# Where the last modulation slabs are computed in a two-layer trunk: two pairs to the second attention, one pair of each attention to its end, lambda arithmetic later in the head

## The reference

```
def layer(x, cond, p, l, angles, ctx):
    mod = jax.nn.silu(cond) @ p['w_mod'][l] + p['b_mod'][l]          # 1024 x 6144 per layer
    sh1, sc1, g1, sh2, sc2, g2 = jnp.split(mod, 6, axis=-1)
    h = rms_norm(x, p['norm1'][l]) * (1.0 + sc1) + sh1
    mixed, ctx_out = token_mixers(h, p, l, angles, ctx)   # attention, linear attention, diff. attention, gated merge
    x = x + g1 * mixed
    h = rms_norm(x, p['norm2'][l]) * (1.0 + sc2) + sh2
    a, u = jnp.split(h @ p['w_ffn_in'][l], 2, axis=-1)
    x = x + g2 * ((jax.nn.silu(a) * u) @ p['w_ffn_out'][l])
# in the differential attention: p = softmax1 - lam * softmax2
#   lam = exp(sum(lp[0]*lp[1])) - exp(sum(lp[2]*lp[3])) + lam_init
```

## Time and profile before

| what | value |
|---|---|
| median of three runs | 2388.95 us (2387.24 to 2390.85) |
| the profiled execution | 2387.86 us, its span 2386.1 us |
| PE busy | 2310.7 us, 97% of the span |
| DVE busy | 1495.4 us, 63% |
| ACT busy | 1065.7 us, 45% |
| DMA | 224.01 MB, mean 94 GB/s |
| granted TensorE clock | 0.992 of full |

### The profile page before, as it was taken

The page is one execution under the profiler, slowest core; times in us unless marked ns, Lnnn a source line. Parts: engine busy times, 40 slices in busy tenths (PEclk is TensorE's granted clock), DMA queues, the critical chain, the costliest instruction groups (busy, mean ns, idle before and its releaser), DMA issues. The chain is left out here.

```text
span 2386.1 us, 40526 instructions
## 1 busy us (share of the span) xinstructions
PE 2310.7 (97%) x16311; PEld 2139.7 (90%) x16311; DVE 1495.4 (63%) x2403; ACT 1065.7 (45%) x2121; POOL 194.7 (8%) x160
## 2 busy tenths in 40 slices
PE   7999999899999999999999999999999999999999
PEld 5877877799999999999997777778999999999998
DVE  5335568677664865747643565787676658467473
ACT  5433357644442642524346333674444345344252
POOL 1330000100003000000215200010000110000000
PEclk9999999999999999999999999999999999999999
DMA  9225440122225223232231163102222432323222
GB/s 299 96 68 172 143 152 28 45 80 80 75 94 159 63 79 88 81 98 68 93 125 53 51 199 120 33 1 71 80 80 80 159 81 73 105 62 98 65 73 84
DMA packets 246666, 224.01 MB, mean 94 GB/s; under 512 B 6945, under 2 KB 232305, under 8 KB 245969
## 3 DMA queue, kind: packets, MB, share of 16 engines
q1 hardware_dynamic: 242528, 219.25, 29.7%
q0 software_dynamic: 480, 0.66, 0.3%
q10 hardware_dynamic: 3472, 1.52, 0.2%
HBM read 211.70 MB, written 9.70 MB: 93 GB/s over the span
## 5 line engine op out<-in xcount | busy, mean ns | idle before, releaser
L2352 ACT ACTIVATE ring_high<-raw 128x512 fp32r<-128x512 f32 (+1 forms) x278 | 158.1, 609 | 250.0 <-PE ps L2706 150.4
L2492 DVE TENSOR_TENSOR ring_low<-raw,ring_high 128x512 fp32r<-128x512 f32 (+1 forms) x278 | 204.5, 761 | 69.3 <-ACT ring_high L2352 65.1
L2771 PE MATMUL ps<-hH,ring_low 128*128 128x320 f32 x640 | 197.9, 309 | 0.3
L2771 PE MATMUL ps<-hH,ring_high 128*128 128x320 f32 x640 | 197.8, 309 | 0.0
L2771 PE MATMUL ps<-hL,ring_high 128*128 128x320 f32 x640 | 197.8, 309 | 0.0
L1564 DVE SCALAR_TENSOR_TENSOR xT<-ps,mod,xT 128x512 f32<-128x512 f32 (+1 forms) x128 | 64.0, 545 | 193.4 <-PE ps L2706 193.4
L359 PE MATMUL ps<-wH,hL 128*128 128x512 f32 (+1 forms) x460 | 176.5, 384 | 5.2 <-DVE wL L871 2.6
L359 PE MATMUL ps<-wH,hH 128*128 128x512 f32 (+1 forms) x460 | 171.0, 372 | 0.0
L2706 PE MATMUL ps<-gH,ring_low 128*128 128x320 f32 x704 | 160.9, 310 | 0.3 <-DVE xT L1564 0.3
L2706 PE MATMUL ps<-gL,ring_high 128*128 128x320 f32 x704 | 160.4, 309 | 0.0
L2706 PE MATMUL ps<-gH,ring_high 128*128 128x320 f32 x704 | 160.3, 309 | 0.0
(11 more groups left out here) (384 smaller groups left out, 6194.8 us busy)
## 6 DMA issues: line engine op xcount, KB each, us to landing
raw<-in_w_in SPq DMA_DIRECT2D x56, 1024.0 KB, 5.4
raw<-in_w_ffn_in SPq DMA_DIRECT2D x88, 512.0 KB, 5.2
gmod<-in_w_mod SPq DMA_DIRECT2D x24, 1024.0 KB, 8.6
raw<-in_w_ffn_out SPq DMA_DIRECT2D x16, 1024.0 KB, 5.1
b_raw<-in_w_branch SPq DMA_DIRECT2D x22, 512.0 KB, 4.4
head_w<-in_w_mod SPq DMA_DIRECT2D x8, 1024.0 KB, 12.4
modw<-in_w_mod SPq DMA_DIRECT2D x8, 1024.0 KB, 7.6
raw<-in_w_out SPq DMA_DIRECT2D x8, 1024.0 KB, 5.8
```

The source lines that it names most:

```text
L2352: nc.scalar.activation(ring_block(m.ring_high, b, src.shape[1], src.shape[2]), src, ACT.Copy).then_inc(m.sem("w_high"), 1)
L2492: nc.vector.tensor_tensor(ring_block(m.ring_low, b, nk, cols), src, ring_block(m.ring_high, b, nk, cols).bitcast(F32), ALU.subtract).then_ ...
L2771: last = nc.tensor.matmul(m.ps[:, plan.banks[n, 0][BANK[what]], 0:HALF], w[:, k, :], a[:, k, :], start=(first and k == 0 and q == 0), stop ...
```

## The change

Four things. The lambda arithmetic moves on DVE and ACT from before slab 2 to before slab 3's place in the loop (its buffer `lpw` gets a place of its own). Layer 1's projections do slabs 8 to 15 only; slabs 16 to 19 become two pairs of layer 1's attention. Each attention ends with a pair (`mod_pair` after the last step) which it leaves in its bank; the merge copies it (`late_row`), turns it behind its first tile, and adds it on DVE before tile b1 may write that bank. So layer 0's fourth pair goes from step 16 to the end, and its turn chunks are (0, 1) at step 5 and (2) at step 11; layer 1 has pair 0 ahead of the steps, its turn at step 2, and pair 1 at the end. Buffers for six slabs instead of four.

```diff
-        self.modw = [at(f"modw{j}", [P, KT, W256], 61440 + (0, 8192, 32768, 40960)[j]) for j in range(4)]
+        self.modw = [at(f"modw{j}", [P, KT, W256], (61440, 69632, 94208, 102400, 0, 8192)[j]) for j in range(6)]
...
+def attention_mods(L):
+    return [(L + 1, slab) for slab in (0, 2, 4, 6)] if L + 1 < DEPTH else [(L, 16), (L, 18)]
...
-    mods = range(8, 20)
+    mods = range(8, 20 if more else 16)
...
-            if more:
-                sp.wait_ge(m.sem("low_ready"), n)
-                for j in range(2):
-                    sp.dma_start(m.modw[j][:, :, :], k_tiles(d["w_mod"], L + 1, j * W256, W256)
-                                 ).then_inc(m.sem(f"attention_mod{j}"), 16)
+            sp.wait_ge(m.sem("low_ready"), n)
+            layer, slab = attention_mods(L)[0]
+            for j in range(2):
+                sp.dma_start(m.modw[j][:, :, :], k_tiles(d["w_mod"], layer, (slab + j) * W256, W256)
+                             ).then_inc(m.sem(f"attention_mod{j}"), 16)
...
-    mod_at = {6 * p - 2: p for p in range(1, pairs)}
-    turn_at = {6 * p - 1: p // 2 for p in range(1, pairs, 2)}
+    pairs = attention_mods(L)
+    buffers = [(0, 1), (2, 3), (4, 5), (4, 5)] if more else [(0, 1), (4, 5)]
+    mod_at = {4: 1, 10: 2} if more else {}
+    turn_at = {5: (0, 1), 11: (2,)} if more else {2: (0,)}
...
+            pe.wait_ge(*freed(len(chunks) - 2))
+            mod_pair(len(pairs) - 1, len(chunks))
...
-            order.step(affine(nc, m, dve, order, L, 1))
             if more:
-                dve.wait_ge(*freed(max(turn_chunk.values())))
-                order.step(affine(nc, m, dve, order, L + 1, 0))
+                order.step(affine(nc, m, dve, order, L, 1))
+    return 6 + len(chunks) % 2
...
@@ merge, ACT @@
             highs(-1)
+            nc.scalar.activation(m.late_row[:, :], m.ps[:, late_bank, 0:W256], ACT.Copy).then_inc(m.sem("late_row"), 1)
             for g in plan.gates:
...
@@ merge, DVE, in the loop over tiles @@
+                    if g == 0 and what == 1:
+                        layer, slab = attention_mods(L)[-1]
+                        dve.wait_ge(m.sem("late_turned"), 1)
+                        summed_late = order.step(sum_mod(nc, m, late_bank, W256, 2, 2))
+                        dve.wait_ge(*summed_late)
+                        add_mod_bias(nc, m, layer, 2 * slab, 2).then_inc(m.sem("late_added"), 1)
+                        dve.wait_ge(m.sem("late_added"), 1)
+                        order.step(affine(nc, m, dve, order, layer, 0 if layer > L else 1))
...
@@ merge, PE @@
                         last.then_inc(m.sem("tile_done"), 1)
+                        if (g, c) == (0, 0):
+                            pe.wait_ge(m.sem("late_row"), 1)
+                            turn_mod(nc, m, m.late_row, late_bank, W256).then_inc(m.sem("late_turned"), 1)
                     for c in range(2):
+                        if (g, c) == (0, 1):
+                            pe.wait_ge(m.sem("late_added"), 1)
                         branch(g, c).then_inc(m.sem("tile_done"), 1)
...
@@ head, ACT @@
-                if n == 1:
+                if n == 3:
                     act.wait_ge(m.sem("lam_sums"), 1)
...
@@ head, DVE: the lambda lines become the function lambdas(), called later @@
             ahead = slabs_ahead(slabs)
             for n in range(N):
+                if n == 3:
+                    lambdas()
                 for x in ahead[n][0]:
```

More of the change, by code:

```diff
@@ L987, in _ @@
             sp.wait_ge(m.sem("caches"), 6 * 16)
-            if more:
-                for j in range(2):
-                    sp.wait_ge(m.sem(f"attention_mod{j}"), 16)
+            for j in range(2):
+                sp.wait_ge(m.sem(f"attention_mod{j}"), 16)
         @block.scalar
@@ L1205, in attention @@
     of_step.append([])
-    if more:
-        add_chunk(0, 0, None, 0, "act")
+    add_chunk(0, 0, None, 0, "act")
     first_mods = of_step.pop()
@@ L1268, in store_values, with load_pair @@
                              m.kv[:, 4:8, CTX, :]).then_inc(m.sem("v_stored"), 16)
[L1270 to L1280, removed]
+            def load_pair(p):
+                layer, slab = pairs[p]
+                for i, b in enumerate(buffers[p]):
+                    sp.dma_start(m.modw[b][:, :, :], k_tiles(d["w_mod"], layer, (slab + i) * W256, W256)
+                                 ).then_inc(m.sem(f"mod_loaded{b}"), 16)
+            for b in buffers[0]:
+                sp.sem_inc(m.sem(f"mod_loaded{b}"), 16)
+            for p in ((1, 2) if more else (1,)):
+                load_pair(p)
+            store_values(sp)
             for j in range(2):
-                next_load(sp, m, nxt, j, *(("slab_used", 2 * pairs - 3 + j) if more else ()))
+                next_load(sp, m, nxt, j, "slab_used", 2)
+            if more:
+                sp.wait_ge(m.sem("slab_used"), 6)
+                load_pair(3)
             next_loaded(sp, m, nxt)
@@ L1349, in mod_pair @@
             def mod_pair(p, c):
-                for i in range(2):
-                    j = 2 * p + i
-                    pe.wait_ge(m.sem(f"mod_loaded{j % 4}"), 16 * (j // 4 + 1))
-                    mod_groups(nc, m, m.modw[j % 4], 6 + c % 2, i).then_inc(m.sem("slab_used"), 1)
+                for i, b in enumerate(buffers[p]):
+                    pe.wait_ge(m.sem(f"mod_loaded{b}"), 16 * sum(b in x for x in buffers[:p + 1]))
+                    mod_groups(nc, m, m.modw[b], 6 + c % 2, i).then_inc(m.sem("slab_used"), 1)
             for c in first_mods:
@@ L1374, in _ @@
                     if turn is not None:
-                        pe.wait_ge(*freed(mod_chunk[2 * turn + 1]))
-                        for i in range(2):
-                            last = turn_mod(nc, m, m.mrow[:, 2 * turn + i, :], 6 + c % 2, i * W256)
+                        pe.wait_ge(*freed(mod_chunk[turn[-1]]))
+                        for i, p in enumerate(turn):
+                            last = turn_mod(nc, m, m.mrow[:, p, :], 6 + c % 2, i * W256)
                     if mod is not None:
@@ L1539, in _ @@
                         if turn is not None:
-                            done = order.step(sum_mod(nc, m, 6 + c % 2, 0, 4, 2))
+                            done = order.step(sum_mod(nc, m, 6 + c % 2, 0, 2 * len(turn), 2))
                             dve.wait_ge(*done)
-                            for i in range(2):
-                                ins = add_mod_bias(nc, m, L + 1, 8 * turn + 4 * i, 2, 8 * i)
+                            for i, p in enumerate(turn):
+                                ins = add_mod_bias(nc, m, pairs[p][0], 2 * pairs[p][1], 2, 8 * i)
                         if n:
@@ L3367, in program @@
             project_attention(nc, m, d, L)
-            attention(nc, m, d, L, (SLAB, lambda sp, j, sem: load_merge(sp, m, d, L, 0, 0, j, sem), 16))
-            merge(nc, m, d, L, (tail_slabs(False)[0], first_slabs, 16))
+            late_bank = attention(nc, m, d, L, (SLAB, lambda sp, j, sem: load_merge(sp, m, d, L, 0, 0, j, sem), 16))
+            merge(nc, m, d, L, (tail_slabs(False)[0], first_slabs, 16), late_bank)
             tail(nc, m, d, L)
```

39 lines of the change are left out of this document (21 added, 18 removed).

## The result

| | before | changed |
|---|---|---|
| median, us | 2388.55 (6 runs) | 2397.39 (6 runs) |
| lowest to highest | 2385.27 to 2390.85 | 2394.12 to 2399.24 |
| profiled execution: time, span | 2387.86, 2386.1 | 2396.26, 2394.5 |

The ratio is 1.0036, with a 95% interval of 1.0026 to 1.0046: the change makes the kernel 8.8 us slower by the medians, 8.4 by the profiled executions. The prediction of 2393.0 had the side right; its range ended at 2396.5. Measured once more in another set, the changed kernel took 2395.45 against 2389.77, a ratio of 1.0026 (1.0015 to 1.0036), 5.7 us slower.

What follows compares the result with a forecast made beforehand. PE's own work and its few waits bound the kernel (97% busy). Terms -4.8 - 2.1 + 6.8 - 1.6 - 0.65 + 6.7 = +4.35 us gave 2393.0, own range 2391 to 2395, with rivals 2389 to 2396.5.

Steps and rivals of the forecast that it cites:

- Head, -4.8: Between slabs 1 and 2, moving lambda removes PE's pause (3.3 us) and the half clock behind it (1.5).
- Merges, +6.8 and +6.7: Layers 0 and 1: PE waits for ACT's late copy, queued behind gate 1's load, with 1.5 us of half clock charged.
- the second new wait: In the merge, PE's wait at b1 for DVE's late addition; claimed not to bind (484.8 against 487.3 in layer 0).
- Projections of layer 1, -1.6: Two pairs go (3.9 us), but a late key store brings a new PE pause of 2.3, leaving 1.6.
- Attention of layer 1, -0.65: Pair 0 fills the pause of 2.19, gaining 1.15 us; the single turn at step 2 costs 0.5.
- Attention of layer 0, -2.1: Pair 3 and the double turn leave (2.6 us); a turn of one pair comes in at 0.5.
- The pair at the attention's end: A last pair of 1.93 us runs while DVE, ACT and POOL finish: costs nothing, at most 0.3 in layer 1.
- (a): Merges: the late copy is in time, costing only 0.35 each; 2377.5 to 2380.5, chance 0.08.
- (b): The clock stays up in the merges' pauses: 3.1 us less, 2390, chance 0.10.
- (c): The store isn't late in layer 1's projections: 2.3 us less, 2390.7, chance 0.13.
- (d): More is lost: slab 2's load late in the head, or turns 0.7 each and longer half clock; 2395 to 2396.5, chance 0.14.
- (e): Head: the lambda move does nothing, as another load holds ACT; +4.8 us, 2398, chance 0.05.

Runs made afterwards that it cites:

- experiment 4: Changed kernel with PE doing 36 discarded matmuls of tile (0,1) while it waits for the late row: 2396.42 us, ratio 1.0035; run again, 2395.36.
- experiment 3: Changed kernel with SP's first store of the differential keys issued ahead of the two modulation loads, both layers: 2391.78 us, ratio 1.0016.
- experiment 5: Changed kernel without the late pair's copy, transposes and DVE work in the merges (output not the reference's): 2382.04 us, ratio 0.9971.
- experiment 2: Changed kernel with only ACT's copy of the late row moved ahead of the blocks that wait for gate 1's load: 2399.66 us, ratio 1.0049.
- experiment 6: Changed kernel with DVE's late addition earlier, and either PE's turn behind tile (0,1) (2380.47 us) or ACT's copy ahead of gate 1's wait (2381.86).
- experiment 1: Kernel before with only the lambda move and its buffer `lpw`: 2384.86 us, ratio 0.9983.

## Why the prediction was right or wrong

The step that failed first is in the projections of layer 1: the pause that the store causes was charged its own length, and the half clock behind it was put at nothing. It follows in six of eight profiles and costs 1.6 us on average. The other misses are two sizes, the turn of one pair and the half clock in the merges, and a gain that was read from a single execution.

**Head, -4.8: right.** The pause went with lambda, 4.85 by the means and 4.3 by the medians of the edit alone. "All but some 0.1" was too sure: in three of twelve executions slab 2's load is late itself.

**Merges, +6.8 and +6.7: the mechanism right, the size low.** The copy ran right behind the two blocks, the pause was 6.26 and 6.29, and moving the copy and the addition took it away. The half clock was charged at the head's 1.5; behind these longer pauses it cost 2.6 and 2.1 on average (experiment 4). With the wait's own length that makes 7.7 and 7.15: 0.9 and 0.45 missed. How much it costs is partly chance: with pauses nearly as long, in experiment 3, the merges lost 6.5 and 6.8, about what was predicted. That the clock kept up in tile (0,0) gains nothing while PE waits anyway was right: it is 1.5 us once the wait is gone (experiment 5). That the second new wait doesn't bind was right as well, but only behind the first (experiment 2).

**Projections of layer 1, -1.6: the step that failed.** "A new pause of 2.3, and 1.6 is left of the gain": the pause came where it was said, for the reason that was said, with 2.58. But it was priced without half clock behind it, while the same text charged it for the merges and pointed to a pause of 2.19 that was followed by it. It follows in six of eight profiles. Over these eight the stage takes 185.4 on average, as the three profiles with the old projections do: nothing is left of the two pairs' 3.9 us. Like against like, both terms that were named are right. Without half clock in the stage it goes from 184.6 to 182.8 and 182.7, a gain of 1.8 to 1.9. With the store first it takes 181.9 and 182.2, against 185.6 and 185.9 before, all four with half clock behind the modulation's pause: 3.7 for the 3.9. Of the loss, the pause was foreseen and 1.6, on average, was not.

**Attention of layer 1, -0.65: the second step that failed.** The 1.15 was read from one profile, in which half clock stood behind the pause of 2.19. Two others with the old attention don't show it (132.4 long), and against these the stage, 133.4, costs 1.0. That pair 0 fits into the pause was right: the maxima up to the sixth stand where they stood. The 1.0 is the single turn, taken as 0.5 between 0 and 0.7 by halving a turn of two pairs. PE's transposes take 0.38, and behind them it waits 0.56 for DVE, which it doesn't behind a turn of two pairs (0.11 at most). Why only the single turn has this wait is open.

**Attention of layer 0, -2.1: 0.45 too much,** for the same price of the turn: there too the maxima behind it come 1.0 later. **The pair at the attention's end** cost under 0.1 in layer 1, where the last maximum comes 1.0 later and the stage is 1.0 longer; the bound was 0.3.

**The rivals.** (a) isn't what happened; experiment 6 made it true by moving the late pair's operations, and 2380.5 and 2381.9 are near its 2380.5. (b) falls: the clock fell in the merges' pauses in all three profiles with the late pair unmoved and PE idle. (c) falls, and the store does what was said. (d) comes nearest, and partly by other items than it named: it had the turns at 0.7 and a longer half clock, and lacked the one behind the store. Its 2396.5, the end of the whole range, lies 0.9 under the measured 2397.39; the other set's 2395.45 lies inside. That is the spread between sets and no merit of the sum, which was too low by 3.6 in the means of the stages. (e) falls by the head's stage and by experiment 1.

What the larger part of the five misses has in common is that it rests on what the clock did behind a pause in one execution; the rest, 0.45 to 0.5 in each attention, is the turn. The prediction charged the half clock where the pause was long, left it out where the pause was a by-product, and counted it as a gain where one profile happened to have it.

## What to carry to other kernels

An operation put behind a wait on its own queue can cost the engine that needs it the whole wait, however small it is; look on each engine for the idle stretch that it fits into, and check all the links of a chain (copy, turn, addition), since moving one alone uncovers the next wait; here two of the three had to move. A small store that something waits for is worth trying ahead of large loads on its queue. When a sum counts the half clock behind one pause, count it behind all, as a chance times its price, and take from several profiles which of the old pauses have it.

## What the runs showed of the hardware

Behind the same pause of some 1.9 us, at the same place of a projection, PE's clock fell in 9 of 26 cases (13 profiles, two layers; twice in layer 0, seven times in layer 1), at a price of 1.0 to 1.8 us each. Behind the pause of 2.19 at the start of the old attention of layer 1 it fell in one of three, behind the store's of 2.4 to 4.0 in six of eight, and behind the late row's of 6.0 to 6.3 in six of six. It also fell in 3 of 11 profiles early in layer 1's new attention, behind pauses of PE of only 0.55 and 0.82, at a price of 1.6 us. That is a part of the spread of some 6 us between the runs of one kernel, whose other part I have not traced.

A store of 128 KB took 1.8 us when SP issued it ahead of two loads of 1 MB, and 7.3 to 9.0 us when SP issued it 0.6 us behind the second of them. The loads themselves took 5.1 to 9.3.
